# Two chained blocks at 256 tokens: the first modulation in quarters, three projections fed by k-quarter, packed dense weights

## What is computed

```python
mod = c_act @ w_ada[l] + b_ada[l]
shift, scale, gate = jnp.split(mod, 3, axis=-1)
h = rmsnorm(x, norm_g[l]) * (1.0 + scale[:, None]) + shift[:, None]
proj = h @ w_in[l]
...
a = jnp.einsum('becd,edf->becf', xs, w_gate)
u = jnp.einsum('becd,edf->becf', xs, w_up)
y = jnp.einsum('becf,efd->becd', jax.nn.silu(a) * u, w_down) * gate[..., None].astype(h.dtype)
```

## Time and profile before

| | |
|---|---|
| median of 3 runs | 1555.35 us (1554.5 to 1555.72) |
| the profiled execution | 1554.04 us, of which the span of instructions is 1552.2 us |
| busy share of the span | TensorE 77%, VectorE 40%, ScalarE 27%, DMA queue of SyncE 86% |
| granted TensorE clock over the span | 0.882 |

### The profile page before, as it was taken

The page is one execution under the profiler, slowest core; times in us unless marked ns, Lnnn a source line. Parts: engine busy times, 40 slices in busy tenths (PEclk is TensorE's granted clock), DMA queues, the critical chain, the costliest instruction groups (busy, mean ns, idle before and its releaser), DMA issues.

```text
span 1552.2 us, 18204 instructions
## 1 busy us (share of the span) xinstructions
PE 1198.4 (77%) x7368; PEld 696.7 (45%) x7368; DVE 614.4 (40%) x1041; ACT 425.8 (27%) x644; POOL 36.9 (2%) x62
## 2 busy tenths in 40 slices
PE   7999999999999999976666665665655665665665
PEld 5888977887887899721111111111111111111112
DVE  3786789889777876511011011011011011110111
ACT  3665357786554674300000000000000000000001
POOL 0000000010001000000000000000000000000000
PEclk9999999999999999988777787787878877777788
DMA  9876877687756666999999999999999999999996
GB/s 362 284 263 216 308 245 246 231 307 235 273 183 209 215 220 245 390 432 430 430 432 430 430 431 432 430 432 432 432 429 431 432 430 431 431 430 430 432 432 276
DMA packets 78323, 550.62 MB, mean 355 GB/s; under 512 B 5032, under 2 KB 5320, under 8 KB 61856
## 3 DMA queue, kind: packets, MB, share of 16 engines
q1 hardware_dynamic: 75168, 541.08, 86.2%
q0 software_dynamic: 2784, 8.08, 1.7%
q10 hardware_dynamic: 288, 0.30, 0.1%
HBM read 548.36 MB, written 1.61 MB: 354 GB/s over the span
## 4 chain that ended last, share of the span: by engine, by line
PE 43%; DMA 36%; DVE 12%; ACT 4%; issue 3%; SPq 0%; DVEq 0%; ACTq 0%; POOL 0%
PE ps L610 41%; DMA b<-in_w_down 34%; DVE b L1535 6%; ACT b L1171 3%; PE ps L614 3%; DVE b L1552 2%; DVE b L2265 1%; ACT b L1173 1%; DVE b L2206 1%; DMA b<-in_w_in 1%; DMA b<-in_w_ada 1%; DVE b L2212 1%; DVE b L1545 0%; ACT L1171 0%; DVE b L1566 0%
## 5 line engine op out<-in xcount | busy, mean ns | idle before, releaser
L610 PE MATMUL ps<-b,b 128*32 128x512 f32 (+7 forms) x6922 | 1130.3, 541 | 300.0 <-DMA b<-in_w_up 117.3
L610 PEld LDWEIGHTS ps<-b,b 128*32 128x32 f32 (+2 forms) x6922 | 640.9, 159 | 750.5 <-issue 456.5
L1171 ACT ACTIVATE b<-ps 128x512 f32<-128x512 f32 (+3 forms) x165 | 92.2, 559 | 868.7 <-PE ps L610 560.7
L1535 DVE TENSOR_TENSOR b<-b,b 128x1024 fp32r<-128x1024 f32 (+5 forms) x254 | 277.1, 1091 | 98.1 <-ACT b L1171 78.9
L1171 ACT ACTIVATE b<-b 128x1024 fp32r<-128x1024 f32 (+6 forms) x219 | 219.1, 1001 | 213.9 <-PE ps L610 161.2
L2255 DVE TENSOR_TENSOR b<-b,ps 128x512 f32<-128x512 f32 x16 | 11.0, 687 | 395.6 <-issue 382.3
L2265 DVE TENSOR_TENSOR b<-b,ps 128x1024 f32<-128x1024 f32 x28 | 34.2, 1222 | 304.3 <-PE ps L610 304.3
L614 PE MATMUL ps<-b,b 128*128 128x128 f32 (+1 forms) x360 | 69.7, 322 | 38.4 <-DVE b L1566 23.5
L614 PEld LDWEIGHTS ps<-b,b 128*128 128x128 f32 (+1 forms) x360 | 45.8, 168 | 88.9 <-DVE b L1566 36.4
L1552 DVE SCALAR_TENSOR_TENSOR b<-b,b,b 128x512 f32<-128x512 f32 (+3 forms) x50 | 63.2, 1263 | 4.3 <-ACT b L1171 0.5
L1535 DVE TENSOR_TENSOR b<-ps,b 128x512 f32<-128x512 f32 (+8 forms) x69 | 37.6, 545 | 26.5 <-PE ps L610 14.9
(11 more groups left out here) (59 smaller groups left out, 201.0 us busy)
## 6 DMA issues: line engine op xcount, KB each, us to landing
b<-in_w_up SPq DMA_DIRECT2D x30, 4096.0 KB, 43.2
b<-in_w_gate SPq DMA_DIRECT2D x29, 4096.0 KB, 43.0
b<-in_w_down SPq DMA_DIRECT2D x29, 4096.0 KB, 38.5
b<-in_w_in SPq DMA_DIRECT2D x73, 1024.0 KB, 5.6
b<-in_w_ada SPq DMA_DIRECT2D x28, 1024.0 KB, 5.5
b<-in_w_gate SPq DMA_DIRECT2D x6, 2048.0 KB, 9.0
...
```

What stands on the lines that cost most here:

```text
L610: return e.matmul(o, lhsT, rhs, start=start, stop=stop, skip_group_check=True)
L1171: e.activation(o, i, f, bias=bias, scale=scale).then_inc(mark[0], 1)
L1535: e.tensor_tensor(o, a, b, op).then_inc(mark[0], 1)
```

## The change

The modulation is made in four quarters of 2 MB instead of two parts of 4 MB; quarter q gives shift and scale for k = 2q and 2q+1, and costs 32 matmuls of 128 columns (where a part cost 32 of 256). The 12 first halves go V0, Q0, V1 for each k-quarter, and their weights come as 0.5 MB transfers in the order ada q, three halves, ada q+1. TensorE makes quarter q+1 after the second half of quarter q, and flips its result inside the third (after that half's first three matmuls). The weights of `w_ada` (shift, scale and gate) and of all dense slots are packed on the host, so that a partition reads 4 or 8 KB in one piece, where it read pieces of 2 KB (4 KB for the gate). `x` is scaled by column halves, token tile 0 by VectorE and 1 by ScalarE; the square of tile 1 moves to VectorE. The products that TensorE makes at the start, with results that nobody uses, take a zeroed buffer, are 24 instead of 10 and no longer wait for the constants. The eight ada chunks of TensorE move two steps back, (3, 3) to (10, 3). Q0's convolution, V0's and V1's copies and the copy of `R1` move with them. At the end one square comes behind the second copy to `YS`.

```diff
-            for i, (which, a) in enumerate((w, a) for a in (0, 2) for w in ("V0", "Q0", "V1")):
-                for j in range(2):
-                    add(which, a + j, a + j == 0, a + j == 3, (s + (2 * i + j) // 4, (2 * i + j) % 4))
+            for i, (a, which) in enumerate((a, w) for a in range(4) for w in ("V0", "Q0", "V1")):
+                add(which, a, a == 0, a == 3, (s + i // 4, i % 4))
...
-ADA_STEP = {(a + 1, 3): a for a in range(NADA_PE)}
+ADA_STEP = {(a + 3, 3): a for a in range(NADA_PE)}
...
@@ SyncE @@
+            def ada0(q):
+
+                for i in range(2):
+                    ks = slice(i * KD // 2, (i + 1) * KD // 2)
+                    src = dram["ada0"][q * P:(q + 1) * P, i * KD // 2 * W:(i + 1) * KD // 2 * W].rearrange("p (k n) -> p k n", n=W)
+                    e.dma_start(ADA0[q][:, ks, :], src).then_inc(S(f"ada0_{q}_{i}"), 16)
+            def first_half(g):
+
+                c, ks = g // 2, slice(2 * (g % 2), 2 * (g % 2) + 2)
+                if c >= RING:
+                    e.wait_ge(S("v_lo"), g - 2 * RING + 1)
+                e.dma_start(ring[c % RING][:, ks, :], dense(c)[:, ks, :]).then_inc(half_landed(g)[0], 16)
...
-            for k in range(0, KD, 2):
-                ada0(0, k)
-            ring_load(0)
-            ring_load(1)
-            for k in range(0, KD, 2):
-                ada0(1, k)
-                if k == 0:
-                    ring_load(2)
+            for q in range(4):
+                ada0(q)
+                for g in range(3 * q, 3 * q + 3):
+                    first_half(g)
@@ TensorE @@
+                            if g in (2, 5, 8) and (t, kk) == (0, 0):
+                                ada0_flip(g // 3 + 1)
...
-            e.wait_ge(S("const_in"), 16)
-            keep_clock(10)
-            e.wait_ge(S("v_xn"), NT)
-            for q in range(4):
-                flip_pair(f"XT{q}", XN, 2 * q)
+            e.wait_ge(S("g_set"), 1)
+            keep_clock(24, with_=ZEROS)
...
-                if (s, c) in ((0, 1), (0, 3)):
-                    for k in (c - 1, c):
-                        ada0(1, k)
+                if g in (1, 4, 7):
+                    for k in range(KD):
+                        ada0(g // 3 + 1, k)
@@ ScalarE @@
-                if (s, c) == (0, 3):
-                    e.wait_ge(*free("R0F1"))
-                    tokens_hi(2)
-                    tokens_hi(3)
+                if g in (2, 5, 8):
+                    tokens_hi(g // 3 + 1)
...
-                for t in range(NT):
-                    e.wait_ge(S("p_sum"), 6 + 2 * t if n else 3 + t)
+                for t, n_ in ((0, 0),) if n == 0 else ((1, 0), (0, 1), (1, 1)):
+                    e.wait_ge(S("p_sum"), 6 + 2 * t if n_ else 3 + t)
@@ VectorE @@
                 lo(g + AHEAD)
 
-                if (s, c) == (0, 2):
-                    modulation(1)
-                    tokens(2)
-                if (s, c) == (0, 3):
-                    modulate_lo("XT2", 1, HTL, HTH)
-                    tokens(3)
-                    modulate_lo("XT3", 1, HTL, HTH)
+                if g in (2, 5, 8):
+                    modulation(g // 3 + 1)
+                    tokens(g // 3 + 1)
+                    tokens_lo(g // 3 + 1)
```

More of the change, by code:

```diff
@@ L190 @@
 LOAD_AT = {what: i for i, what in enumerate(LOADS)}
+assert LOADS[:NFIRST // 2] == [("w", c) for c in range(NFIRST // 2)]
 SLACK, CONTEXT_DONE, KEYS_DONE = (next(g // 2 for g in range(0, NHALF, 2) if HALVES[g][4] == (SLOT[n], 0)) for n in ("PA0", "V2b", "CB"))
@@ L536, in expert_load @@
                 e.dma_start(o, chunk_src(n)).then_inc(landed_, 16)
-            for i in range(3, len(LOADS) - 1):
+            for i in range(NFIRST // 2, len(LOADS) - 1):
                 if LOADS[i] == ("w", SLACK):
@@ L868, in _, with ada0_flip @@
-            ada0_flips(0)
-            keep_clock(6)
+            def ada0_flip(q):
+                begin(f"R0F{q}")
+                e.wait_ge(*free(f"R0{q}"))
+                flip(ps[:, 6, 0:P], MOD0[q]).then_inc(FULL[6], 1)
+            e.wait_ge(S("v_first"), 1)
+            for k in range(4):
+                ada0(0, k)
+            e.wait_ge(S("const_in"), 16)
+            for n in range(2):
+                e.wait_ge(S("v_first"), 2 + n)
+                e.wait_ge(S("a_xn"), 1 + n)
+                flip_pair(f"XT{2 * n}", XN, 4 * n)
+                if n == 0:
+                    flip_pair("XT1", XN, 2)
+                    for k in range(4, KD):
+                        ada0(0, k)
@@ L871, in _ @@
+            ada0_flip(0)
+            flip_pair("XT3", XN, 6)
+            keep_clock(3)
             for g, ts in UNITS:
@@ L1255, in _, with tile_copied @@
             e.wait_ge(S("x_in"), 16)
-            for t in range(NT):
-                act(XJ[:, t, :], X[:, t, :], ACT.Square, accum=csq[:, t:t + 1], to=S("a_xsq"))
-            for q in range(4):
+            act(XJ[:, 0, :], X[:, 0, :], ACT.Square, accum=csq[:, 0:1], to=S("a_xsq"))
+            e.wait_ge(S("g_pow"), 1)
+            for n in range(2):
+                copy(XN[:, 1, n * W:(n + 1) * W], X[:, 1, n * W:(n + 1) * W], scale=csq[:, 1:2], to=S("a_xn"))
+            def tile_copied(q):
                 e.wait_ge(*full(f"XT{q}"))
                 copy(XTS[:, q, :], ps[:, 2 + q, :], to=free(f"XT{q}"))
+            tile_copied(0)
             def tokens_hi(q):
+                e.wait_ge(*free(f"R0F{q}"))
+                e.wait_ge(*free(f"XT{q}"))
                 for i in range(2):
@@ new lines, in _ @@
+            copy(crep2[:, :, 16:32], cst[:, 2 * KD:3 * KD].unsqueeze(2).broadcast_to([P, KD, 16]), to=S("v_first"))
+            e.wait_ge(S("x_in"), 16)
+            e.wait_ge(*order.behind)
+            mark = order.mark(None)
+            e.scalar_tensor_tensor(out=XJ[:, 1, :], in0=X[:, 1, :], scalar=1.0, in1=X[:, 1, :], op0=ALU.mult, op1=ALU.mult,
+                                   accum_out=csq[:, 1:2]).then_inc(mark[0], 1)
+            order.behind = mark
+            e.wait_ge(S("a_xsq"), 1)
@@ new lines, in _, with tile_copied, modulation @@
+            rstd(0, csq, D)
+            for n in range(2):
+                ts(XN[:, 0, n * W:(n + 1) * W], X[:, 0, n * W:(n + 1) * W], csq[:, 0:1], None, ALU.mult, to=S("v_first"))
+            def tile_copied(q):
+                e.wait_ge(*full(f"XT{q}"))
+                copy(XTS[:, q, :], ps[:, 2 + q, :], to=free(f"XT{q}"))
+            tile_copied(1)
+            l4, neglam = lam4.rearrange("p (a b) -> p a b", a=4), lamv[:, 0:1]
+            def modulation(q):
+                e.wait_ge(*full(f"R0{q}"))
+                copy(MOD0[q], ps[:, 7, 0:P], to=free(f"R0{q}"))
+                e.wait_ge(*full(f"R0F{q}"))
+                v = ps[:, 6, 0:P].rearrange("p (n j) -> p n j", n=4)[:, :, 0]
+                gs, sh, bsc, bsh, gain = (a[:, 2 * q:2 * q + 2] for a in (
+                    GS, SH, part(cols, COLS, "b_sc"), part(cols, COLS, "b_sh"), part(cols, COLS, "norm_g")))
+                tt(gs, v[:, 2:4], bsc, ALU.add)
+                stt(gs, gs, 1.0, gain, ALU.add, ALU.mult)
+                tt(sh, v[:, 0:2], bsh, ALU.add, to=free(f"R0F{q}"))
@@ L1698, in _ @@
             lo(0)
-            modulate_lo("XT0", 1, HTL, HTH)
-            tokens(1)
-            modulate_lo("XT1", 1, HTL, HTH)
-            for g in (1, 2):
-                lo(g)
+            tokens_lo(0)
+            lo(1)
+            tile_copied(3)
+            lo(2)
             def conv(name, dst, c0, i):
```

165 lines of the change are left out of this document (73 added, 92 removed).

## The result

| | before | after |
|---|---|---|
| median, 20 runs each | 1555.24 us | 1559.3 us |
| the profiled execution | 1554.04 us, span 1552.2 | 1558.48 us, span 1556.7 |
| granted TensorE clock over the span | 0.882 | 0.874 |

The ratio after to before is 1.0025, 95% interval 1.0018 to 1.0033. The change makes the kernel 0.25% slower, clear of the noise; 1552.6 us, 0.18% faster, was forecast, in a range from 1550.6 to 1556.0.

What follows compares the result with a forecast made beforehand. TensorE's dense phase was taken to set when the byte-bound expert stream starts: 4.4 us earlier less 2.0 for returning chunks, plus 0.6 at the end, less 0.2 for waits, saves 2.8: median 1552.6 us, range 1550.6 to 1556.0.

Steps and rivals of the forecast that it cites:

- the rival of costly quarters: Modulation quarters: each takes 3.5 us, two add 3.3 us, total 1555.9, no change; chance 0.13.
- the reading by 64 records: Modulation quarters: some 62 ns decoding per matmul record makes a quarter 4.0 us and the total 1556.8.
- w22 stayed hidden: Slots 9 to 12: weight load w22, issued behind ada chunk A6, lands at 174.8, hidden with 3.5 us to spare.
- The end: Last copy to YS: with ScalarE's square behind it, it starts 0.6 us earlier, and all behind it.
- 24.5 + 1.06 + 0.05 + 1.23 + 0.1 + 0.25 = 27.2: Half 2: from half 5's landing to VectorE's copy of quarter 1, for which TensorE's flip waits until 27.2 us.
- rest of half 2, 9/12 of 2.72 and a flip, 2.2: Half 2 behind quarter 1's flip: remaining matmuls and a flip take 2.2 us, part of 31.5 us to half 11's end.
- the -4.4 forecast: Start of half 12, the first half the same before and after: at 61.7 instead of 66.13, 4.4 us earlier.
- the first milestone: Start of half 12, at 66.13 us in the kernel before, forecast at 61.7 us.
- SyncE's queue behind w22 (A7, A11, w23) slips too, under the same cover: Slots 9 to 12: loads queued behind w22 come later but stay hidden, as w22 does with 3.5 us to spare.
- the third rival: Ring loads: w22 lands at 178.7, TensorE waits 3.7 us, w24 repeats it, up to 7 us, 1559.6; chance 0.07.
- 0.2 us for slots 9 to 12: Slots 9 to 12: allowance for small waits, taken off the 3.0 us saving to leave 2.8.
- the rival of the clock: Clock fall at 126.4 to 129.8, costing about 1.6 us, is gone: 4.4 us saved, 1551.0; chance 0.17.

Runs made afterwards that it cites:

- e4b: Changed kernel with 40 idle products on TensorE ahead of the flip inside half 2; ratio to the kernel before 1.0024.
- e4c: Changed kernel with 20 idle products on TensorE ahead of the flip inside half 2; ratio to the kernel before 1.0009.
- e2: Changed kernel with TensorE's eight ada chunks at steps (2,3) to (8,3), none left in slots 9 and 10; ratio to the kernel before 1.0015.
- e3: Changed kernel with e2's chunk places and modulation and tokens of quarters 1 to 3 ahead of lo(3), lo(8), lo(11); ratio to the kernel before 0.9994.
- e9: e3 with the tokens' lo of quarters 2 and 3 also put ahead of lo(8) and lo(11); ratio to the kernel before 0.9985.
- e10: e9 with GpSimd's small loads (decay, lam, gate weights) released after 7 lo instead of 10; 1552.03 us, ratio to the kernel before 0.9982.
- r1_before: The kernel before, unchanged, profiled once more; span 1551.8 us, no ratio timed.
- r1_after: The changed kernel, unchanged, profiled once more; span 1556.0 us, no ratio timed.
- e1: Changed kernel with quarter 1's modulation and tokens on VectorE ahead of lo(3), its tokens' lo behind lo(3); 1556.07 us, ratio to the kernel before 0.9999.
- e5: Changed kernel with all dense weights loaded from the original arrays in 2 KB pieces, modulation quarters still packed; ratio to the kernel before 1.0021.
- e6: Kernel before with only the eight ada chunks moved to (3,3) to (10,3) and the copy of their sum to (11,0); ratio 1.0000.

## Why the prediction was wrong

**What held.** The mechanism at the start: the flip of quarter 1 waits for VectorE's copy behind lo(3) to lo(5), and lo(5) for the last load; the flips in halves 5 and 8 hardly wait. A quarter takes 1.9 us (21.95 to 23.83 between the halves), so 128 columns cost what they should, and the rival of costly quarters falls, with the reading by 64 records (4.0 us). Packing gives 412 GB/s in the start (0.5 MB in 1.27 us), for 415 taken. w22 stayed hidden (landed at 173.0, 174.8 worked out). The end gives 0.6 us. The stream runs at 431 GB/s.

**The first step that failed: "24.5 + 1.06 + 0.05 + 1.23 + 0.1 + 0.25 = 27.2".** The flip came at 29.26. 1.8 us of it is the load: `hi(5)` starts at 26.30. The rate was right, but the landings of half 1 (14.78) and half 2 (17.48) are 2.7 us apart, 1.4 more than the others, and half 0 had landed 0.4 later than forecast. The trace of before has a gap like it, 2.69 us for 0.5 MB behind the first weights (18.94 to 21.63), that the estimate did not read. The queue moved 1.14 MB in that gap (422 GB/s), so it was not idle; why no transfer ended in it stays open.

**The second: "rest of half 2, 9/12 of 2.72 and a flip, 2.2".** That is the price at the upper clock. It took 4.1 us (29.26 to 33.35), and half 3 behind it 3.1 instead of 2.7. The clock that the standstill costs was left out of the sum, though the wait was in it (3.4 us forecast, 4.45 idle measured): 2.3 us in this execution, shown by e4b and e4c. With 0.8 us in small pieces these two make the 4.9 us between the -4.4 forecast and the +0.50 measured at the first milestone.

**The third: "SyncE's queue behind w22 (A7, A11, w23) slips too, under the same cover".** It was w23 and not w22 that had no cover: three transfers and GpSimd's queue in 12.4 us. The mechanism is that of the third rival, one load further: the mLSTM product behind a late lo. It cost 1.2 us of standstill and some 0.5 more, where the sum had 0.2 us for slots 9 to 12. e2, e3, e9 and e10, in which those chunks stand elsewhere, have none of it.

**A fourth, of which the sum had nothing: the load of half 88.** From hi(84) to hi(92) the changed kernel lost 0.9 us in its first trace and 2.6 in its second; the kernel before lost nothing in either.

**The draws.** That the fall of the earlier trace rows was gone gave 1.5 us in this execution, which is what the rival of the clock said. But r1_before has no such fall without the change, so it is a draw and not the change's gain, as the prediction's own argument against that rival had it. The fall at 198 took some 1.7 to 1.9 us; r1_after has none, yet only kernels that wait there show one, so a part of it may be the change's in the median.

**What the change costs and brings, then.** Up to hi(22) two chunks' time (2.0 us) is moved away and the wait for the first weights shortened, and a standstill and the clock behind it are paid: +0.5 is left in the first pair of traces and -1.8 in the second (r1_after against r1_before), for -4.4 forecast. The two chunks come back (2.0) with a wait (1.4 to 2.1), the load of half 88 costs 0.9 to 2.6, the end gives 0.6. The spans differ by 4.5 us in the first pair and 4.2 in the second, the medians by 4.1. So the sign of the change hangs on the start, which did not save what it should; with e1's order of the start, and the rest of the change as it was, the ratio is 0.9999.

Why the load of half 88 took 5.8 us here, 7.5 in r1_after and e9 and 4.9 in both traces of before is not settled. e3 and e10, packed too, have 5.1 and 5.4; two executions of the changed kernel differ by 1.7 us; e5 and e6 (0.96 and 0.7 us lost there) say that neither long pieces nor the new start is needed for it. It runs beside GpSimd's load of `ctx`. That load in the changed kernel, in the kernel before and in e9:

```profile
b<-in_dense SPq DMA_DIRECT2D x1, 1024.0 KB, 5.8
```

```profile
b<-in_w_in SPq DMA_DIRECT2D x1, 1024.0 KB, 4.9
```

```profile
b<-in_dense SPq DMA_DIRECT2D x1, 1024.0 KB, 7.5
```
